# An encoder block on one core: block sums of w_down made by GpSimd on chip, and the up projection's result moved by DMAs

## The reference

```python
x = x + mixed @ w_o                      # 256 x 2048
h = rms_norm(x, norm_ffn)                # eps 1e-5
u = h @ w_up                             # 2048 x 11264: gate columns, then value columns
up = pad(u, two rows of zeros ahead)
c = conv_b + sum(up[:, j:j + S] * conv_w[j] for j in range(3))
gate, val = c[..., :5632], c[..., 5632:]
x = x + (silu(gate) * val) @ w_down      # 5632 x 2048
return rms_norm(x, norm_final)
```

## Time and profile before

| | us |
|---|---|
| three runs | 1037.18, 1037.89, 1038.49 (median 1037.89) |
| span of the profiled execution, first to last instruction | 1035.4 |
| TensorE busy in it | 1026.6 |
| VectorE busy | 793.9 |
| ScalarE busy | 734.5 |
| GpSimd busy | 88.9 |
| mean DMA rate over the span | 258 GB/s |

### The profile page before, as it was taken

The page is one execution under the profiler, slowest core; times in us unless marked ns, Lnnn a source line. Parts: engine busy times, 40 slices in busy tenths (PEclk is TensorE's granted clock), DMA queues, the critical chain, the costliest instruction groups (busy, mean ns, idle before and its releaser), DMA issues.

```text
span 1035.4 us, 15993 instructions
## 1 busy us (share of the span) xinstructions
PE 1026.6 (99%) x5141; PEld 858.3 (83%) x5141; DVE 793.9 (77%) x1026; ACT 734.5 (71%) x1191; POOL 88.9 (9%) x150
## 2 busy tenths in 40 slices
PE   9999999999999999999999999999999999999997
PEld 8888888888888888888888888888888878888885
DVE  5679787887767578768687787876868999887677
ACT  6966474745556687988879888798887766646664
POOL 1000000000111111111111111111111000000000
PEclk9999999999999999999999999999999999999999
DMA  9676767667899999898999998989999589888993
GB/s 295 188 225 178 238 189 224 191 208 215 271 285 321 282 290 269 264 266 278 264 288 254 280 263 269 282 254 278 261 274 264 167 306 316 295 289 285 319 313 113
DMA packets 156103, 266.85 MB, mean 258 GB/s; under 512 B 11908, under 2 KB 60388, under 8 KB 155936
## 3 DMA queue, kind: packets, MB, share of 16 engines
q1 hardware_dynamic: 138224, 222.67, 65.7%
q0 software_dynamic: 17360, 43.22, 18.9%
q10 hardware_dynamic: 480, 0.47, 0.1%
HBM read 256.86 MB, written 44.06 MB: 291 GB/s over the span
## 4 chain that ended last, share of the span: by engine, by line
PE 98%; DMA 1%; SPq 0%; DVE 0%; ACT 0%; issue 0%; DVEq 0%
PE pj L1523 12%; PE pj L1528 12%; PE pj L1524 12%; PE pj L1536 9%; PE tr_ps L1528 9%; PE tr_ps L1523 9%; PE tr_ps L1524 9%; PE pj L1541 5%; PE sc_ps L1528 4%; PE sc_ps L1523 4%; PE sc_ps L1524 4%; PE pj L1558 3%; PE pj L1551 2%; PE pj L1517 1%; PE pj L1519 1%; PE pj L1518 1%
## 5 line engine op out<-in xcount | busy, mean ns | idle before, releaser
L1000 DVE TENSOR_TENSOR split<-raw,split 128x1024 fp32r<-128x1024 f32 x265 | 321.6, 1222 | 159.6 <-ACT split L641 153.8
L641 ACT ACTIVATE split<-raw 128x1024 fp32r<-128x1024 f32 x259 | 272.7, 1056 | 125.1 <-PE pj L1528 26.0
L929 ACT ACTIVATE split<-raw 128x1024 fp32r<-128x1024 f32 (+1 forms) x125 | 121.6, 989 | 63.6 <-PE sc_ps L1528 27.9
L1335 DVE TENSOR_TENSOR split<-raw,split 128x1024 fp32r<-128x1024 f32 (+1 forms) x125 | 138.2, 1136 | 31.0 <-ACT split L929 29.3
L1523 PE MATMUL tr_ps<-split,act_split 128*128 128x512 f32 x352 | 136.9, 389 | 0.0
L1524 PE MATMUL tr_ps<-split,act_split 128*128 128x512 f32 x352 | 136.9, 389 | 0.0
L1523 PE MATMUL pj<-split,act_split 128*128 128x512 f32 x352 | 136.9, 389 | 0.0
L1524 PE MATMUL pj<-split,act_split 128*128 128x512 f32 x352 | 136.9, 389 | 0.0
L1536 PE MATMUL pj<-act_split,split 128*128 128x512 f32 x416 | 131.6, 398 | 0.0
L1528 PE MATMUL tr_ps<-split,act_split 128*128 128x512 f32 x352 | 94.1, 389 | 0.0
L1528 PE MATMUL pj<-split,act_split 128*128 128x512 f32 x352 | 94.1, 389 | 0.0
(11 more groups left out here) (249 smaller groups left out, 1660.9 us busy)
## 6 DMA issues: line engine op xcount, KB each, us to landing
raw<-w_up SPq DMA_DIRECT2D x176, 512.0 KB, 5.8
raw<-w_in SPq DMA_DIRECT2D x72, 512.0 KB, 4.3
raw<-w_down SPq DMA_DIRECT2D x68, 512.0 KB, 6.0
t_dram<-w_down POOLq DMA_DIRECT2D x60, 512.0 KB, 6.6
raw<-t_dram SPq DMA_DIRECT2D x40, 512.0 KB, 6.0
raw<-w_o SPq DMA_DIRECT2D x32, 512.0 KB, 6.3
t_dram<-t_dram POOLq DMA_DIRECT2D x40, 256.0 KB, 6.6
raw<-w_down SPq DMA_DIRECT2D x20, 256.0 KB, 6.1
```

Source lines behind the costliest of these rows:

```text
L641: ins = act.activation(hi[:, slot, 0:TILE], raw[:, slot, 0:TILE], ACT.Copy)
L929: act.activation(hi[:, slot, c0:TILE], down_raw(t)[:, c0:TILE], ACT.Copy).then_inc(hi_done, 1)
L1000: dve.tensor_tensor(lo[:, slot, 0:n], raw[:, slot, 0:n], hi[:, slot, 0:n].bitcast(F32), ALU.subtract).then_inc(lo_done, 1)
L1335: dve.tensor_tensor(lo[:, slot, c0:TILE], down_raw(t)[:, c0:TILE], hi[:, slot, c0:TILE].bitcast(F32), ALU.subtract).then_inc(lo_done, 1)
```

## The change

Two edits at once. (1) The DMAs that made sums in DRAM are gone. SyncE loads both full halves of a unit (`b1`, `b2`), and GpSimd adds blocks in SBUF straight into the raw slots of the unit's third and fourth tile: four additions of 128x512 for each unit, beside the down stage. The load into a slot that held b1 or b2 waits until the unit's sums are made (`raw_free`). (2) ScalarE copies an up step's result with two instructions into `token_u`, tokens still on their partitions and scaled there by `r2c`; 16 DMAs on SyncE's queue move the blocks between partition quarters; VectorE turns them with two instructions. The token order of `act_hi`/`act_lo` changes to fit, and the final gain's load goes from GpSimd's queue to SyncE's.

```diff
+def loaded(t):
+    return DOWN[t][1] == "plain" or DOWN[t][2] < 2
+def raw_free(t):
+    last = raw_before(t)[-1]
+    kind, part = DOWN[last][1:3]
+    return last, sums_index(last - part) + 1 if kind == "sums" and part < 2 else 0
+MOVE_AT = 2
+LAST_MOVE_AT = 8
+GFIN_AFTER = 12
# SyncE
+            def move_u(j, v):
+                sp.wait_ge(evac_u, step_of(j, v, 1, 1))
+                for a in range(SIDE):
+                    for b in range(SIDE):
+                        sp.dma_start(moved[b * BLOCK:(b + 1) * BLOCK, a], token_u[a * BLOCK:(a + 1) * BLOCK, b]).then_inc(d_mv, 16)
             def up_loads(j, first):
                 for v in range(2):
                     for kt in range(UP_TILES):
+                        if not first and kt == MOVE_AT:
+                            move_u(j - 1, v)
...
             for t, (g, kind, part, kt) in enumerate(DOWN):
+                if t in (MOVE_AT, LAST_MOVE_AT):
+                    move_u(UP_PAIRS - 1, (MOVE_AT, LAST_MOVE_AT).index(t))
+                if t == GROUP_END[0] + GFIN_AFTER:
+                    sp.wait_ge(z_s, 8)
+                    sp.dma_start(gfin[:], norm_final.partition_broadcast(P)).then_inc(d_gf, 16)
+                if not loaded(t):
+                    continue
...
+                    last, sums_made = raw_free(t)
+                    sp.wait_ge(lo_done, T_DOWN + last + 1)
+                    if sums_made:
+                        sp.wait_ge(t42_s, 2 * sums_made)
# GpSimd (the five DMAs per unit by way of DRAM are removed)
+            def weight_sums(j):
+                t = UNITS[j]
+                b1, b2 = down_raw(t), down_raw(t + 1)
+                t13, t42 = down_raw(t + 2), down_raw(t + 3)
+                left, right = slice(0, 512), slice(512, TILE)
+                for n in range(2):
+                    pool.wait_ge(d_w[raw_slot(t + n)], slot_loads(t + n))
+                for n in range(2, 4):
+                    if raw_before(t + n):
+                        pool.wait_ge(lo_done, T_DOWN + raw_before(t + n)[-1] + 1)
+                    else:
+                        pool.wait_ge(glo_s, UP_PAIRS)
+                    if raw_slot(t + n) < RING:
+                        pool.wait_ge(lo_done, T_DOWN)
+                if j > 0:
+                    pool.wait_ge(t42_s, 2 * j)
+                pool.tensor_tensor(t13[:, left], b1[:, left], b2[:, left], ALU.add).then_inc(t13_s, 1)
+                pool.tensor_tensor(t13[:, right], b2[:, left], b2[:, right], ALU.add).then_inc(t13_s, 1)
+                pool.wait_ge(t13_s, 2 * j + 1)
+                pool.tensor_tensor(t42[:, right], b2[:, right], t13[:, left], ALU.add).then_inc(t42_s, 1)
+                pool.wait_ge(t42_s, 2 * j + 1)
+                pool.tensor_tensor(t42[:, left], b1[:, right], t42[:, right], ALU.add).then_inc(t42_s, 1)
# ScalarE
+            def evacuate_u(j, v):
+                act.wait_ge(mm_done, step_of(j, v, UP_TILES, T_UP + UP_TILES))
...
+                for m in range(MT):
+                    ins = act.activation(token_u[:, :, m].rearrange("p b w i -> p w b i"),
+                                         up_banks[v][:, m].rearrange("p (w b i) -> p w b i", w=4, b=SIDE), ACT.Copy, scale=r2c[:, m:m + 1])
+                ins.then_inc(evac_u, 1)
             def conv_first(j, v, pair):
-                act.wait_ge(u_s, step_of(j, v, 2, pair + 1))
+                act.wait_ge(u_s, step_of(j, v, 2, 2))
             def finish(j, v, s):
-                if s in MOVES:
-                    ins = move_blocks(...)
+                if s == 0:
+                    evacuate_u(j, v)
# VectorE
             def turn_moved(j, v):
-                dve.wait_ge(moved_s, step_of(j, v, 1, 1))
+                dve.wait_ge(d_mv, step_of(j, v, PARTS_U, PARTS_U))
...
-                st.done(dve.transpose(ub[:, :, 2:S + 2], moved[:].rearrange("p w m a i -> p w (m a i)")))
-            def scale_rows(): ...
+                for m in range(MT):
+                    dve.transpose(ub[:, :, m * P + 2:(m + 1) * P + 2].rearrange("p w (a x) -> p w a x", a=SIDE),
+                                  moved[:, :, m].rearrange("p a w i -> p w a i")).then_inc(u_s, 1)
```

More of the change, by code:

```diff
@@ L94, in raw_before @@
     return [s for s in range(t) if raw_slot(s) == raw_slot(t)]
+def loaded(t):
+    return DOWN[t][1] == "plain" or DOWN[t][2] < 2
 def slot_loads(t):
     slot = raw_slot(t)
[L100 to L112, removed]
+    return (T_DOWN // RING * 16 + (32 if slot % 2 == 0 else 0) if slot < RING else 0) + 16 * (sum(map(loaded, raw_before(t))) + 1)
+def raw_free(t):
+    last = raw_before(t)[-1]
+    kind, part = DOWN[last][1:3]
+    return last, sums_index(last - part) + 1 if kind == "sums" and part < 2 else 0
+UNITS = [t for t, d in enumerate(DOWN) if d[1:3] == ("sums", 0)]
 WO_ORDER = [(0, 0), (0, 1), (0, 2), (0, 4), (0, 5), (0, 6), (1, 0), (1, 1), (1, 2), (1, 4),
@@ L316, in program @@
         d_w = [sem(f"d_w{i}") for i in range(RING + EXTRA)]
-        t_done = [sem(f"t_done{i}") for i in range(2)]
-        tsum_s = sem("tsum_s")
+        t13_s, t42_s = sem("t13_s"), sem("t42_s")
         d_x = [sem(f"d_x{i}") for i in range(4)]
@@ L619, in _ @@
                 pool.tensor_copy(fq[:], fcum[:, :, bass.ds(j * 4, 4)]).then_inc(fq_s, 1)
-            for turn in range(TSUM_TURNS):
-                weight_sums(turn)
-            pool.wait_ge(z_s, 8)
-            pool.dma_start(gfin[:], norm_final.partition_broadcast(P)).then_inc(d_gf, 16)
+            for j in range(len(UNITS)):
+                weight_sums(j)
         @block.scalar
@@ L944, in _ @@
                     down_hi(t + LEAD)
[L945 to L948 removed]
+                if t == 0:
+                    evacuate_u(*last_step)
                 if t == 1:
                     silu_gate(UP_PAIRS - 1)
[L951 to L953 removed]
+                if t in (5, 6):
+                    conv_first(*last_step, t - 5)
+                if t == 9:
                     gated_hi(UP_PAIRS - 1)
@@ L1343, in add_values @@
                     dve.wait_ge(s_fp, 4 * q)
+                else:
+                    dve.wait_ge(u_s, 4 * UP_PAIRS)
                 dve.wait_ge(glo_s, kt // 2 + 1)
@@ L1407, in gain @@
                                          gfin[:, n * 512:(n + 1) * 512], ALU.mult)
-            def move_blocks(first, last):
-                for i in range(first, last):
-                    a, b = divmod(i, SIDE)
-                    rows = up_banks[1][a * BLOCK:(a + 1) * BLOCK].rearrange("p m (w b i) -> p m w b i", w=4, b=SIDE)[:, :, :, b]
-                    dve.tensor_copy(moved[b * BLOCK:(b + 1) * BLOCK, :, a % 2, a // 2::2].rearrange("p w m i -> p m w i"), rows).then_inc(moved_d, 1)
-            half = SIDE * SIDE // 2
-            dve.wait_ge(mm_done, T_DOWN)
             for t in range(DOWN_END):
-                if t == 2:
-                    dve.wait_ge(moved_d, half)
-                if t == 2:
+                if t == 4:
                     turn_moved(UP_PAIRS - 1, 1)
```

157 lines of the change are left out of this document (39 added, 118 removed).

## The result

The changed kernel takes 1207.3 us (median of four runs, 1206.55 to 1207.73), the kernel before 1037.7: a ratio of 1.163 (95% interval 1.1613 to 1.1646), 169.6 us slower. Forecast were 1082, with 1118 as the upper end.

The account below looks back on a forecast made before the run. TensorE, busy 1026.6 of 1035.4 us, was taken to bound the kernel; 1037.9 plus 44 for the block sums (35 + 9) and 0 for the up projection gave 1082 us, range 1044 to 1118.

Parts of the forecast that it names:

- No gain possible, sign: Whole kernel: TensorE is busy 1026.6 of 1035.4 us, so nothing beyond a few tenths of us can be gained; faster 0.02.
- The two engines take turns, read off three copies, at 1.03 us per addition: Down stage: VectorE's two-input splits and GpSimd's additions read SBUF one at a time, each addition holding VectorE up 1.03 us.
- Sum of the block sums, 35 + 9: Down stage: additions stall TensorE by 35.4 us in the first column group and 9 in the second, together 44.
- the plain sum: Down stage, per group: 41.2 us of additions less VectorE's free time, 5.8 us in the first, 22.2 in the second.
- head start: Second column group: plain tiles and raw slots let its first unit be made early, taking 10 us off its 19.
- second side: Down stage: load and four additions as a chain, 11.5 us per unit with turns; 32 us in the first group.
- Rival A: Down stage: additions cost VectorE nothing, only the chain of load and additions counts: +4, 1042, up to 1071; chance 0.16.
- The up projection, cost 0: Up projection: 16 moves at 0.34 us per issue, landing 2.9, leave tile 7's lo split 1.5 us early; cost 0.
- rival C: Up projection: SyncE's 16 issues at 0.62 us make the turn 3 us late per step: +63, 1145; chance 0.17.
- The load behind the moves has 16 us to spare: Up projection: this load goes out some 3 us late but has about 16 us from issue to TensorE's use.
- The last moves, zero to 3: Start of the down stage: the last moves stand ahead of load 8 and the turn; zero, up to 3 us.
- Loads land sooner without the DRAM traffic: Down stage: with GpSimd's DMAs by way of DRAM gone, a load lands in 3.7 us, against 6.0 for w_down.

Follow-up runs that it names:

- memset_once: sums_only with each GpSimd addition replaced by one memset of the same columns, waits and loads kept (output not the reference's): 1036.6 us.
- sums_only: The kernel before with the first edit alone, block sums added on GpSimd in SBUF, up projection as before: 1107.2 us.
- spare_adds: The kernel before plus a chain of four GpSimd additions per unit whose result nobody reads or waits for: 1073.5 us.
- memset_twice: sums_only with each GpSimd addition replaced by two memsets, all waits kept (output not the reference's): 1046.0 us.
- four_moves: The changed kernel with four DMAs of 128 KB per up step in place of its 16 moves, same bytes and place: 1143.7 us.

## Why the prediction was wrong, step by step

- **No gain possible, sign:** right. memset_once, free of both costs, shows the floor: 1036.6.
- **The two engines take turns, read off three copies, at 1.03 us per addition:** right in mechanism and nearly in size. An addition costs VectorE 1.05 to 1.10 us; on GpSimd it takes 1.27 where no split is in its way.
- **Sum of the block sums, 35 + 9:** 40 and 30 were measured in sums_only. The step that failed is "the plain sum" for the second group: additions less VectorE's free time, less 10 us of head start. As the price of alternating alone it was close: spare_adds, where nobody waits for a sum, lost 32 and 6. But VectorE is idle for 32 of 80 us in the second group and TensorE waits all the same, because the chain of load and additions sets the pace: GpSimd waits 3.7 to 4.0 us for a load between units, and its additions meet splits when they come. From the third unit of a group on, units with one plain tile between them start 10.7 to 11.3 us apart there (at 1098.01 and 1108.75, for one pair) and 10.1 to 11.9 in the first group, against TensorE's 7.5. The prediction had this chain (11.5 us) as its second side, and held it against the first group only. Applied to both groups, less the head start of 10, it gives 32 + (32 - 10) = 54. Most of the other 16 lies in two more terms, as sums_only shows. The head start was 1.4 us and not 10: the first unit of the second group starts 25.1 us after the last of the first, where TensorE's own distance is 4.8 + 8 x 2.72 = 26.5. And the second unit starts 15.6 us after the first, 8 over TensorE's 7.5, where 3 were put. Rival A's case, the chain without alternating, is near memset_twice: +8 was measured, where rival A had +4.
- **The up projection, cost 0:** this is the step that failed most. Two sizes were off: an issue is 0.63 us, not 0.34 (rival C's figure), and landing 1.9, not 2.9. But the method was the larger error. The prediction read times off an undisturbed step and compared one arrival with one deadline. Even at its own price (5.4 + 2.9 = 8.3 us from the moves' start to the turn) the step would probably have been late: four_moves has 7.1 and 8.6 there in the mean and lost 33 us. The moves' time adds to VectorE's work in a loop, 16.1 us of it, so only 21.8 - 16.1 = 5.7 us were free.
- **Rival C, +63 and in all 1145:** right in place, too small, since it priced the first lateness (3 us) and not what the late turn puts off: the splits behind it, the load behind those, the next moves.
- **The load behind the moves has 16 us to spare:** wrong. Blocked for 10 us with nobody waiting for the moves it costs 61.
- **The last moves, zero to 3:** the down stage is 4 us longer than in sums_only (300.9 against 296.9).
- **Loads land sooner without the DRAM traffic:** right in direction; 4.5 us, not 3.7.

## What to carry over

Before an instruction that waits is put on an in-order queue, follow the wait round: if what it waits for depends, over any queue, on what stands behind it, the times add up to a loop whose length has to stay below the step, and slack read from an undisturbed step does not show it. Count issues, not bytes: four DMAs did the work of 16, and the place on the queue mattered as much as the count. Free time of an engine is worth only what lies where the other engine wants it.

## What the runs showed of the hardware

- Sixteen back-to-back SBUF-to-SBUF DMAs of 32 partitions take 10.0 us of SyncE's queue (median 0.59 each), four of 128 KB 2.5 us (0.60): the price goes by the issue. GpSimd's queue takes 0.50 each.
- Four moves of 128 KB land in 5.1 us, sixteen of 32 KB in 1.9, both beside weight loads.
- A GpSimd addition of 128x512 and a VectorE subtraction of two SBUF tiles of 128x1024 alternate where both engines have work: 2.24 us from addition to addition, in place of 1.14 from split to split.
- A GpSimd write without a read (memset 128x512, 0.53 us) costs VectorE's two-input splits nothing: they stay at 1221 ns.
